# Linear attention mixer: the second value block in split form, and some low parts moved in VectorE's order

## The chip, the cores and the metric

The kernel runs on one core of one Trainium2 chip. The metric is device time in microseconds (us) of one execution, median of several; lower is better. The kernel is written by hand for the five engines: TensorE (PE), VectorE (DVE), ScalarE (ACT), GpSimd (POOL) and SyncE (SP), each with its own instruction list, ordered by semaphores. Weights come from HBM by DMAs that SP issues in a fixed order.

## What is computed

The reference is a stack of blocks on 256 tokens of width 1024 in float32: an mLSTM mixer, a mixture of experts (MoE, 16 experts), a gated linear attention mixer (GLA), a second MoE, then a pooling layer, two SwiGLU layers and an attention layer. The change is in the GLA mixer:

```
z = x @ w_in
q, k, v, r, glr = jnp.split(z, [qk, 2 * qk, 2 * qk + D_MODEL, 2 * qk + 2 * D_MODEL], axis=-1)
loga = log_sigmoid(glr @ gate_w + gate_b) / GLA_TAU
o_fwd = gla_chunked(q, k, v, loga[:, :, 0])          # A[t,s] = sum_d q k exp(b_t - b_s), then A @ v
o_bwd = flip_seq(gla_chunked(flip_seq(q), flip_seq(k), flip_seq(v), flip_seq(loga[:, :, 1])))
o = head_norm(o_fwd + o_bwd, norm_g)
return (jax.nn.silu(r) * o) @ w_out
```

## The kernel before

**Split form.** A float32 product can be made in two ways here. *Plain*: the float32 operands go to TensorE as they are; each such product of 128x512 stands as two records in the trace. *By parts*: ScalarE rounds a weight chunk (128x1024) to a high part (`hi`, line 862), VectorE subtracts to get the low part (`lo`, line 867), and TensorE adds three faster products: high by high, high by low, low by high (`PARTS`). The split activations are there from the stage's start. A chunk's parts live in one of three buffers: 0 and 1 in `w_hi`/`w_lo`, 2 in `h_hi`/`h_lo`. `hi` of a chunk waits until TensorE is done with the chunk that had its buffer (`Mixer.free`, counted by `chunk_done`), and `lo` waits for `hi`; TensorE waits for `lo` (`split_ready`).

**Value blocks.** v and r are four blocks of 512 columns, m = 0 to 3 (v, v, r, r). Each has two weight units of 1 MB (the two halves of the contraction), a unit being two chunks. `project(n)` makes half of the work of block m = n // 2. Blocks in `WHOLE_SPLIT` (0 and 3) are made by parts only, by `both_tiles`: four chunks, two for each `project`. Blocks 1 and 2 use their first unit plain (`plain_rows`, line 1847) and their second unit by parts (`split_rows`, line 1860): two chunks for the whole block. The mixer has 28 chunks: 0 to 7 for q and k, 8 to 11 block 0, 12 and 13 the second half of block 1, 14 and 15 of block 2, 16 to 19 block 3, and 20 to 27 the output product.

**Levels.** The attention matrix is built in eight levels, for distances 1, 2, 4, ... 128. For each level n, VectorE computes arguments (`args(n)`, lines 2108 and 2110), ScalarE takes their exponents (line 2032, two instructions), VectorE multiplies them with keys and queries (`key_query(n)`, line 2121), TensorE makes the small products (`level(n)`, line 1904, the last one line 1924), and VectorE copies the wanted entries (`merge(n)`, line 2129, for n < 5; later levels are merged by ScalarE). The two factors of a level lie in one of two buffers, so `args(n + 2)` waits until TensorE has made level n. VectorE's order was, for each n: `key_query(n + 1)`, `merge(n)`, `args(n + 2)`, then one or two low parts. TensorE's order is `project(n)`, `level(n)`.

**SP.** `mixer_sync` loads the mixer's 16 units, then `moe_sync(sp, 1)` follows in the same queue: it loads the next MoE's weights, 1 or 2 MB at a time, each into slots that something has to leave first. Slots of the mixer's units are left by `unit_done`; others by the end of the levels (`lv_psum`), by the head norm (`hcenter_done`), by the last chunks (`chunk_done`). From then on MoE weights stream through the same slots as its matmuls (line 1513, 1557) leave them. The queue is in order: a load that waits holds back all behind it.

Of the kernel before, what the change touches and what calls it, by code (L numbers as in the profile page):

```python
# [31 lines left out]
P = 128  # L32
SEQ, D = 256, 1024
NT = SEQ // P
KD = D // P
# [20 lines left out]
NF = D_FF // P  # L56
# [179 lines left out]
def program(nc, a, out):  # L236

    ctx = ExitStack()
    with ctx:
# [3 lines left out]
        def sem(name):  # L243
            return ctx.enter_context(nc.semaphore(name))
# [92 lines left out]
        gla_u = [st.unit((GLA_ORDER[n % 10],)) for n in range(16)]  # L337
# [16 lines left out]
        hi_ready, split_ready, chunk_done = sem("hi_ready"), sem("split_ready"), sem("chunk_done")  # L354
# [480 lines left out]
                nc.vector.tensor_tensor(xT_lo3[:, c, t], zT[:, c, t], xT_hi3[:, c, t].bitcast(F32),  # L835
                                        ALU.subtract).then_inc(xlo_ready, 1)

        MIX_CHUNKS, GLA_CHUNKS, FFN_CHUNKS = 32, 28, 3 * NF
        chunk0, chunks = {}, 0
        for name, count in (("ml", MIX_CHUNKS), ("gla", GLA_CHUNKS), ("ffn0", FFN_CHUNKS), ("att", MIX_CHUNKS),  # L840
                            ("ffn1", FFN_CHUNKS)):
# [14 lines left out]
        def split_hi(act, u, g, raw, buf, at, first=False, free=None):  # L856

            act.wait_ge(slot_landed[u.slot], u.landed_at(g))
            if not first:
                act.wait_ge(chunk_done, at - 1 if free is None else free)  # L860
            dst = split_buffer(0, buf).rearrange("p (k n) -> p k n", k=raw.shape[1])
            nc.scalar.activation(dst, raw, ACT.Copy).then_inc(hi_ready, 1)  # L862
# [6 lines left out]
        class Mixer:  # L869
# [25 lines left out]
            def hi(self, act, *chunks):  # L895
                for c in chunks:
                    split_hi(act, self.units[c // 2], 0, self.raw(c), self.buffer(c), self.at + c, first=self.at + c < 3,
                             free=self.free(c))

            def lo(self, dve, *chunks):  # L900
                for c in chunks:
                    split_lo(dve, self.raw(c), self.buffer(c), self.at + c)
# [63 lines left out]
            def token_chunk(self, pe, c, banks, operand=None, onto=False, tiles=range(NT)):  # L966

                self.products(pe, c, [(ps[banks[i]][:, :], slice(k2 * HALF, (k2 + 1) * HALF),
                                       (slice(None), c % 4 * 2 + k2, slice(i * P, (i + 1) * P)),
                                       not onto and c % 4 * 2 + k2 == 0, c % 4 * 2 + k2 == KD - 1, False)  # L970
                                      for i in tiles for k2 in range(2)], operand, more=tiles == (0,))

            def token_first(self, pe, banks, operand):
# [70 lines left out]
        ml_mix = Mixer(ml_u, 2, chunk0["ml"])  # L1044
# [642 lines left out]
        def moe_sync(sp, m):  # L1687
            def wait_slot(u):
                if u.lag is not None:
                    sp.wait_ge(unit_done, u.free_at())  # L1690
                elif u.slot == CONST_SLOT and m == 0:
                    sp.wait_ge(const_ready, 3)
                    sp.wait_ge(chunk_done, ml_mix.done(15))
                elif u.slot == CONST_SLOT:
                    sp.wait_ge(ga_psum, 1)
                elif u.slot in (SPARE_SLOT, 11):
                    sp.wait_ge(hcenter_done, HEADS * NT * (m + 1))
                    sp.wait_ge(*((num_psum, HEADS * NT), (go_psum, NT))[m])
                elif u.slot == 12:
                    sp.wait_ge(*((num_psum, HEADS * NT), (go_psum, NT))[m])  # L1700
                elif u.slot in ARENA_SLOTS and m:
                    sp.wait_ge(lv_psum, len(LEVELS))
                elif u.slot == 13:
                    sp.wait_ge(bc_psum, HEADS)
                elif u.slot == 14:
                    sp.wait_ge(gate_rows, 2)
                elif u.slot == LATE_SLOT and m == 0:
                    sp.wait_ge(cols_ready, 1)
                    sp.wait_ge(lam_ready, 1)
                    sp.wait_ge(sc_psum, HEADS)  # L1710
                elif u.slot == LATE_SLOT:
                    sp.wait_ge(lv_psum, len(LEVELS))
                elif u.slot == 10:
                    sp.wait_ge(chunk_done, (ml_mix.done(29), gla_mix.done(25))[m])
                elif u.slot in SPLIT_SLOTS:
                    sp.wait_ge(chunk_done, chunk0[("ml", "gla")[m]] + (MIX_CHUNKS, GLA_CHUNKS)[m])
                elif u.slot == XT_SLOT:
                    sp.wait_ge(xT_taken, m + 1)
# [13 lines left out]
            def load_half(u, src, h):  # L1732
                wait_slot(u)
                load(u, src[:, h * SLOT:(h + 1) * SLOT])
# [17 lines left out]
            for g in range(NGROUP):  # L1752
# [3 lines left out]
                for q in range(2):  # L1756
# [16 lines left out]
                    for c in range(2):  # L1773
# [32 lines left out]
        lv_psum, lv_done, go_psum = sem("lv_psum"), sem("lv_done"), sem("go_psum")  # L1806


        gla_mix = Mixer(gla_u[0:6] + gla_u[7:10:2] + gla_u[10:16], 2, chunk0["gla"],
                        {c: -c % 3 for c in range(10, GLA_CHUNKS)})  # L1810
        HALF_FIRST = (8, 12, 14, 16)
        WHOLE_SPLIT = (0, 3)

        def gla_tensor(pe, gen):

# [36 lines left out]
            def split_rows(n, start):  # L1852

                m, i = n // 2, n % 2
                for c in (HALF_FIRST[m], HALF_FIRST[m] + 1):
                    pe.wait_ge(split_ready, gla_mix.at + c + 1)
# [10 lines left out]
            def both_tiles(m, n):  # L1867

                c = HALF_FIRST[m] + n
                pe.wait_ge(split_ready, gla_mix.at + c + 1)  # L1870
# [10 lines left out]
            def project(n, parts=range(2)):  # L1881
                m, i = n // 2, n % 2
                if n == 6:
                    pe.wait_ge(gv_ready, 2)
                if m in WHOLE_SPLIT:
                    for part in parts:
# [67 lines left out]
        def gla_scalar(act):  # L1954
            hi = gla_mix.hi
# [58 lines left out]
            def value_rows(m):  # L2014

                if m in WHOLE_SPLIT:
                    act.wait_ge(chunk_done, gla_mix.done(HALF_FIRST[m] + 3))
                else:
                    act.wait_ge(unit_done, gla_u[5 + 2 * m].done_at())
                for i in range(NT):  # L2020
                    src = ps[V_BANKS[2 * m + i]][:, :]
                    if m < 2:
                        nc.scalar.activation(gl_v[:, i, m * HALF:(m + 1) * HALF], src, ACT.Copy).then_inc(gv_ready, 1)
                    else:
                        nc.scalar.activation(gl_r[:, i, (m - 2) * HALF:(m - 1) * HALF], src, ACT.Silu).then_inc(gr_ready, 1)
# [3 lines left out]
            for n in range(len(LEVELS)):  # L2029
                for w in range(2) if n else (1,):  # L2030
                    act.wait_ge(e_arg, n + 1)
                    nc.scalar.activation(gl_E[:, n % 2, w, :], gl_E[:, n % 2, w, :], ACT.Exp,
                                         scale=(2 * w - 1) / TAU).then_inc(e_exp, 1)
                if n == 0:
                    key_rows(1)
                    hi(act, 9, 10)
                elif n == 1:
                    hi(act, 11, 12, 13)
                elif n in (2, 4):
                    value_rows(n // 2 - 1)  # L2040
                    hi(act, 12 + n)
                elif n == 3:
                    hi(act, 15)
                elif n == 5:
                    hi(act, 17, 18)
                elif n == 6:
                    near_blocks()
                    block_merge(5)
                    hi(act, 19)
                else:  # L2050
                    block_merge(6)
                    value_rows(2)
                    block_merge(7)
                    value_rows(3)
                    hi(act, 20, 21)
            head_std(act, 1, 0)
            head_scale(act, 1, 0)
            head_std(act, 1, 1)
            zT_scalar(act, 1, 0, xT3, lambda k: mix_cols[:, 8 + k:9 + k])
            head_scale(act, 1, 1)  # L2060
            hi(act, 22)
            zT_scalar(act, 1, 1, xT3, lambda k: mix_cols[:, 8 + k:9 + k])
            hi(act, *range(23, 28))

        def gla_vector(dve, link):
            lo = gla_mix.lo
# [46 lines left out]
            def key_query(n):  # L2113
                dve.wait_ge(e_exp, 2 * n + 1)
                dve.wait_ge(gq_ready, 2)
                if n == 0:
                    factor, rows = gl_E[:, 0, 1, :], gl_q
                else:
                    dve.wait_ge(gk_ready, 2)
                    factor, rows = gl_E[:, n % 2].rearrange("p w c -> p (w c)"), gl_kq  # L2120
                nc.vector.tensor_tensor(factor, factor, rows, ALU.mult).then_inc(qd_ready, 1)
# [19 lines left out]
            for n in range(len(LEVELS)):  # L2141
                if n + 1 < len(LEVELS):
                    key_query(n + 1)
                if n < BLOCK_LEVEL:
                    merge(n)
                if n + 2 < len(LEVELS):
                    args(n + 2)
                if n < 6:
                    lo(dve, *((12, 13), (14,), (15,), (16,), (17, 18), (19,))[n])
            lo(dve, 20, 21)  # L2150
            for i in range(NT):
                dve.wait_ge(go_psum, i + 1)
                for h in range(HEADS):
# [7 lines left out]
                for h in range(1, HEADS):  # L2161
                    head_center(i, h, go_bank(i, h), gl_r)
            zT_vector(dve, 1, 0, xT3)
            lo(dve, 22)
            zT_vector(dve, 1, 1, xT3)
            lo(dve, *range(23, 28))

        def gla_sync(sp):
            mixer_sync(sp, gla_u, a["gla_w_in"][0], a["gla_w_out"][0], 2)
# [1012 lines left out]
```

## Time and profile before

| | |
|---|---|
| median of 3 runs | 1666.49 us (1665.84 to 1667.23) |
| the profiled execution | 1665.51 us, its span 1663.7 us |
| mean granted TensorE clock | 0.906 |
| busy share of the span | PE 79%, DVE 40%, ACT 27%, POOL 1% |
| HBM read | 534.17 MB, 323 GB/s over the span |
| GLA mixer | about 582 to 701 us of the span; its levels 605 to 663 us |
| second MoE | its matmuls from 718 us on |

The page gives busy time by engine and the chain of work that ended last, and the trace gives start and duration of every instruction. Start times are us from the span's start. Matmul durations are modelled and overlap, so the pace of TensorE is read from start to start; VectorE's and ScalarE's instructions overlap by about 0.1 us in the same way.

### The profile page before, as it was taken

Reading aid. Unit: us, or ns where it says so; the run is one execution under the profiler, and the core shown is the slowest. Engines: PE = TensorE matmul, PEld = TensorE weight load, DVE = VectorE, ACT = ScalarE, POOL = GpSimd, SP = SyncE. Lnnn points to the kernel's source line nnn. Section 1 sums busy time; section 2 is a strip of 40 time slices with the busy share of each in tenths; the row PEclk is TensorE's granted clock in tenths of the full one; section 3 lists DMA queues with packets and bytes.
Section 4 is the critical chain, followed back from the end, with each engine's and each line's share of the span. In section 5 each row is a group of like instructions: output and inputs, shape, how many; then the busy total and the mean of one; then the engine's idle time right before and its main releaser. Section 6 shows DMA issues by size and latency. Waiting matters only on the chain.

```text
span 1663.7 us, 20954 instructions
## 1 busy us (share of the span) xinstructions
PE 1321.7 (79%) x8638; PEld 850.4 (51%) x8638; DVE 661.7 (40%) x1083; ACT 449.0 (27%) x728; POOL 23.4 (1%) x47
## 2 busy tenths in 40 slices
PE   9999665376465899993754646669999999999997
PEld 8786121121121486841211212117888889888886
DVE  5664000000010288620100000005877678887767
ACT  4452000000000266510000000003444455654443
POOL 2000000000000100000000000000000000000000
PEclk9999887787797999997977977879999999999999
DMA  9778999999999974899999999999655763075550
GB/s 364 216 295 330 432 430 429 431 430 428 431 431 428 399 283 159 326 369 430 430 430 430 430 430 431 429 428 393 241 176 202 251 203 127 1 254 176 202 202 25
DMA packets 130856, 537.91 MB, mean 323 GB/s; under 512 B 8180, under 2 KB 71924, under 8 KB 103004
## 3 DMA queue, kind: packets, MB, share of 16 engines
q1 hardware_dynamic: 126480, 530.08, 79.7%
q10 hardware_dynamic: 2380, 2.31, 0.9%
q0 software_dynamic: 1920, 4.43, 0.8%
q8 instruction: 57, 0.93, 0.2%
q14 instruction: 19, 0.16, 0.0%
HBM read 534.17 MB, written 2.62 MB: 323 GB/s over the span
## 4 chain that ended last, share of the span: by engine, by line
PE 52%; DMA 38%; DVE 5%; ACT 2%; issue 1%; SPq 1%; DVEq 0%; ACTq 0%
PE bank L951 12%; PE bank L2355 9%; DMA ring<-in_moe_w_down 8%; DMA arena<-in_moe_w_down 7%; DMA xT_pair<-in_moe_w_up 7%; PE bank L2393 7%; DMA moe_slots<-in_moe_w_down 5%; PE bank L2359 5%; PE bank L1513 5%; PE bank L1557 5%; DMA ring<-in_moe_w_up 5%; DMA moe_slots<-in_moe_w_up 5%; DMA arena<-in_moe_w_up 2%; PE bank L589 1%; PE bank L2322 1%
## 5 line engine op out<-in xcount | busy, mean ns | idle before, releaser
L1513 PE MATMUL bank<-ring,arena 128*32 128x512 f32 x960 | 214.6, 713 | 72.5 <-DMA arena<-in_moe_w_up 36.1
L867 DVE TENSOR_TENSOR w_lo<-ring,w_hi 128x1024 fp32r<-128x1024 f32 x151 | 183.0, 1221 | 87.2 <-ACT w_hi L862 86.5
L1557 PE MATMUL bank<-ring,arena 128*32 128x512 f32 x496 | 145.3, 711 | 55.5 <-DMA moe_slots<-in_moe_w_down 22.9
L862 ACT ACTIVATE w_hi<-ring 128x1024 fp32r<-128x1024 f32 x151 | 158.6, 1057 | 82.7 <-PE bank L951 37.8
L2355 PE MATMUL bank<-xT_parts,w_hi 128*128 128x512 f32 x496 | 177.1, 399 | 0.0
L1676 DVE TENSOR_TENSOR arena<-arena,bank 64x512 f32<-64x512 f32 x32 | 22.1, 691 | 384.5 <-ACT arena L1616 384.5
L1513 PE MATMUL bank<-moe_slots,arena 128*32 128x512 f32 x352 | 104.9, 749 | 59.5 <-DMA ring<-in_moe_w_up 33.3
L2359 PE MATMUL bank<-xT_parts,w_lo 128*128 128x256 f32 x496 | 139.1, 280 | 0.0
L1513 PE MATMUL bank<-arena 128*32 128x512 f32 x488 | 106.6, 713 | 24.7 <-DMA ring<-in_moe_w_up 14.8
L1616 ACT ACTIVATE arena<-bank 64x512 f32<-64x512 f32 x32 | 18.8, 588 | 394.6 <-PE bank L1513 394.6
L1513 PEld LDWEIGHTS bank<-ring,arena 128*32 128x32 f32 x960 | 48.9, 127 | 148.4 <-issue 134.4
L1557 PE MATMUL bank<-arena 128*32 128x512 f32 x208 | 74.9, 785 | 49.5 <-DMA moe_slots<-in_moe_w_down 25.0
L2355 PEld LDWEIGHTS bank<-xT_parts,w_hi 128*128 128x128 f32 x496 | 93.2, 188 | 23.4 <-DVE w_lo L867 0.7
L1685 DVE COPY arena<-bank 128x512 f32<-128x512 f32 x8 | 5.5, 692 | 243.3 <-PE bank L1557 243.3
L1557 PE MATMUL bank<-xT_pair,arena 128*32 128x512 f32 x128 | 63.4, 708 | 45.2 <-DMA ring<-in_moe_w_down 45.2
L2359 PEld LDWEIGHTS bank<-xT_parts,w_lo 128*128 128x128 f32 x496 | 93.6, 189 | 0.7
L1624 ACT ACTIVATE arena<-bank 128x512 f32<-128x512 f32 x8 | 4.8, 597 | 317.4 <-PE bank L1557 317.4
L951 PE MATMUL bank<-w_hi,xT_parts 128*128 128x512 f32 x264 | 84.8, 395 | 1.3 <-DVE xT_parts L833 1.2
L1513 PEld LDWEIGHTS bank<-moe_slots,arena 128*32 128x32 f32 x352 | 25.5, 133 | 114.4 <-issue 112.9
L1557 PEld LDWEIGHTS bank<-ring,arena 128*32 128x32 f32 x496 | 33.2, 128 | 92.0 <-issue 89.4
L1557 PE MATMUL bank<-moe_slots,arena 128*32 128x512 f32 x160 | 73.4, 737 | 0.0
L2355 PE MATMUL bank<-xT_parts,f_hi 128*128 128x512 f32 x176 | 63.1, 398 | 0.0
(381 smaller groups left out, 2480.2 us busy)
## 6 DMA issues: line engine op xcount, KB each, us to landing
ring<-in_moe_w_up SPq DMA_DIRECT2D x24, 2048.0 KB, 38.7
ring<-in_moe_w_down SPq DMA_DIRECT2D x22, 2048.0 KB, 40.0
ring<-in_moe_w_gate SPq DMA_DIRECT2D x20, 2048.0 KB, 40.0
moe_slots<-in_moe_w_gate SPq DMA_DIRECT2D x18, 2048.0 KB, 36.9
arena<-in_moe_w_up SPq DMA_DIRECT2D x14, 2048.0 KB, 37.9
arena<-in_moe_w_gate SPq DMA_DIRECT2D x12, 2048.0 KB, 38.7
ring<-in_w_gate SPq DMA_DIRECT2D x22, 1024.0 KB, 5.1
ring<-in_w_up SPq DMA_DIRECT2D x22, 1024.0 KB, 5.2
```

The lines of the kernel that those rows point to most:

```text
L589: nc.tensor.matmul(ps[bank][:, at:at + P], ident, ident, start=True, stop=True)
L862: nc.scalar.activation(dst, raw, ACT.Copy).then_inc(hi_ready, 1)
L867: nc.vector.tensor_tensor(lo, raw, hi.bitcast(F32), ALU.subtract).then_inc(split_ready, 1)
L951: last = nc.tensor.matmul(dst, *(ops if weights_first else ops[::-1]), start=(start and p == 0), stop=(stop and p == 2))
L1513: last = nc.tensor.matmul(ps[B_GU[j % 2]][32 * c:32 * c + 32, :], xin[:, j, k, :], w, start=(k == 0), stop=(k == KD - 1), tile_position=(0 ...
L1557: last = nc.tensor.matmul(ps[B_DN[c]][32 * j:32 * j + 32, :], hT[:, j // 2, at:at + CAP], slot_row(ud[j], f % 2)[:, c * HALF:(c + 1) * HAL ...
L1616: nc.scalar.activation(hmid[64:128, j // 2, :].rearrange("p (r m) -> p r m", r=4), by_row(ps[B_GU[j % 2]][0:64, :]), ACT.Silu).then_inc(si ...
L1676: nc.vector.tensor_tensor(hmid[64 * (j % 2):64 * (j % 2) + 64, j // 2, :].rearrange("p (r m) -> p r m", r=4), hmid[64:128, j // 2, :].rear ...
L2322: return nc.tensor.matmul(FIRST_HALF[n], w[:, k * P:(k + 1) * P], x[:, k, :], start=start, stop=stop)
L2355: both = nc.tensor.matmul(gate_up_bank(f, n)[:, :], w[0][:, k * P:(k + 1) * P], xT_both[:, :, k, :], start=(k == 0), stop=False)
L2359: last = nc.tensor.matmul(gate_up_half(f, n, 1), w[1][:, k * P:(k + 1) * P], xT_hi3[:, k, :], start=False, stop=(k == KD - 1))
L2393: last = nc.tensor.matmul(acc(i, c), h_parts[hp][:, 2 * s + f, i * P:(i + 1) * P], w[wp][:, c * HALF:(c + 1) * HALF], start=False, stop=False)
```

## The change

Block 1 is made by parts as a whole, like blocks 0 and 3: its first unit is now two chunks too, 30 in all (12 to 15 are block 1, 16 and 17 the second half of block 2, 18 to 21 block 3, 22 to 29 the output). The buffers of chunks are counted from the new end, from chunk 11 on. ScalarE's list has two more high parts, and `value_rows(1)` stands after the high part of chunk 17. VectorE's list has two more low parts; those of chunks 15, 17, 19 and 21 stand right after `key_query(n + 1)`, before `merge` and `args`, for n = 2, 3, 5 and 6. The others stand after `args`.

```diff
-        MIX_CHUNKS, GLA_CHUNKS, FFN_CHUNKS = 32, 28, 3 * NF
+        MIX_CHUNKS, GLA_CHUNKS, FFN_CHUNKS = 32, 30, 3 * NF
...
             def token_chunk(self, pe, c, banks, operand=None, onto=False, tiles=range(NT)):
-                                       (slice(None), c % 4 * 2 + k2, slice(i * P, (i + 1) * P)),
-                                       not onto and c % 4 * 2 + k2 == 0, c % 4 * 2 + k2 == KD - 1, False)
+                                       (slice(None), (c - self.count) % 4 * 2 + k2, slice(i * P, (i + 1) * P)),
+                                       not onto and (c - self.count) % 4 * 2 + k2 == 0, (c - self.count) % 4 * 2 + k2 == KD - 1,
+                                       False)
...
-                    sp.wait_ge(chunk_done, (ml_mix.done(29), gla_mix.done(25))[m])
+                    sp.wait_ge(chunk_done, (ml_mix.done(29), gla_mix.done(27))[m])
...
-        gla_mix = Mixer(gla_u[0:6] + gla_u[7:10:2] + gla_u[10:16], 2, chunk0["gla"],
-                        {c: -c % 3 for c in range(10, GLA_CHUNKS)})
-        HALF_FIRST = (8, 12, 14, 16)
-        WHOLE_SPLIT = (0, 3)
+        gla_mix = Mixer(gla_u[0:8] + gla_u[9:16], 2, chunk0["gla"],
+                        {c: (GLA_CHUNKS - 1 - c) % 3 for c in range(11, GLA_CHUNKS)})
+        HALF_FIRST = (8, 12, 16, 18)
+        WHOLE_SPLIT = (0, 1, 3)
...
-                elif n in (2, 4):
-                    value_rows(n // 2 - 1)
-                    hi(act, 12 + n)
+                elif n == 2:
+                    value_rows(0)
+                    hi(act, 14)
                 elif n == 3:
-                    hi(act, 15)
+                    hi(act, 15, 16)
+                elif n == 4:
+                    hi(act, 17)
+                    value_rows(1)
                 elif n == 5:
-                    hi(act, 17, 18)
+                    hi(act, 18, 19)
                 elif n == 6:
                     near_blocks()
                     block_merge(5)
-                    hi(act, 19)
+                    hi(act, 20, 21)
                 else:
                     block_merge(6)
                     value_rows(2)
                     block_merge(7)
                     value_rows(3)
-                    hi(act, 20, 21)
+                    hi(act, 22, 23)
...
             for n in range(len(LEVELS)):
                 if n + 1 < len(LEVELS):
                     key_query(n + 1)
+                lo(dve, *{2: (15,), 3: (17,), 5: (19,), 6: (21,)}.get(n, ()))
                 if n < BLOCK_LEVEL:
                     merge(n)
                 if n + 2 < len(LEVELS):
                     args(n + 2)
-                if n < 6:
-                    lo(dve, *((12, 13), (14,), (15,), (16,), (17, 18), (19,))[n])
-            lo(dve, 20, 21)
+                lo(dve, *{0: (12, 13), 1: (14,), 2: (16,), 4: (18,), 5: (20,)}.get(n, ()))
+            lo(dve, 22, 23)
```

The remaining chunks of the output product are renumbered by two in both lists.

## Rows read from the trace of the kernel before

**Rows 1.** The page: the chain that ended last, by engine.
```profile
PE 52%; DMA 38%; DVE 5%; ACT 2%; issue 1%; SPq 1%; DVEq 0%; ACTq 0%
```

**Rows 2.** The chain that ended last, in order of time: start, length, what.
```profile
748.03 38.04 DMA ring<-in_moe_w_down
```

**Rows 3.** Timeline of VectorE: start, length, engine, line, operation, tiles, idle before.
```profile
615.48 1.23 DVE L867 TENSOR_TENSOR w_lo<-ring,w_hi 128x1024 fp32r<-128x1024 f32 x1 [1.62 <-ACT w_hi L862]
...
617.08 2.29 DVE L2121 TENSOR_TENSOR arena<-arena 128x2048 f32<-128x2048 f32 x1
...
624.16 2.28 DVE L2121 TENSOR_TENSOR arena<-arena 128x2048 f32<-128x2048 f32 x1
626.36 0.44 DVE L2129 COPY_PREDICATED glr_w<-lvl_mask,bank 128x256 f32<-128x256 uint8 x1
626.69 1.22 DVE L2108 TENSOR_TENSOR arena<-y 128x1024 f32<-128x1024 f32 x1
627.83 1.22 DVE L2110 TENSOR_TENSOR arena<-y 128x1024 f32<-128x1024 f32 x1
628.96 1.22 DVE L867 TENSOR_TENSOR w_lo<-ring,w_hi 128x1024 fp32r<-128x1024 f32 x1
631.12 2.29 DVE L2121 TENSOR_TENSOR arena<-arena 128x2048 f32<-128x2048 f32 x1 [0.94 <-ACT arena L2032]
...
649.86 2.35 DVE L867 TENSOR_TENSOR w_lo<-ring,w_hi 128x1024 fp32r<-128x1024 f32 x2
652.13 2.28 DVE L2121 TENSOR_TENSOR arena<-arena 128x2048 f32<-128x2048 f32 x1
...
658.76 2.29 DVE L2121 TENSOR_TENSOR arena<-arena 128x2048 f32<-128x2048 f32 x1 [0.94 <-ACT arena L2032]
```

**Rows 4.** Timeline of ScalarE, the same columns.
```profile
611.55 1.06 ACT L862 ACTIVATE h_hi<-ring 128x1024 fp32r<-128x1024 f32 x1 [1.26 <-PE bank L1874]
...
614.41 1.99 ACT L862 ACTIVATE w_hi<-ring 128x1024 fp32r<-128x1024 f32 x2
...
629.08 2.01 ACT L2032 ACTIVATE arena<-arena 128x1024 f32<-128x1024 f32 x2 [3.15 <-DVE arena L2110]
```

**Rows 5.** Timeline of TensorE, the same columns.
```profile
614.22 0.39 PE L1874 MATMUL bank<-w_lo,xT_parts 128*128 128x512 f32 x1
...
622.17 3.70 PE L1847 MATMUL bank<-ring,xT_pair 128*128 128x512 f32 x8
...
628.57 0.76 PE L1904 MATMUL bank<-arena 128*32 128x32 f32 x64
629.26 0.73 PE L1860 MATMUL bank<-w_hi,xT_parts 128*128 128x512 f32 x2
...
653.43 0.61 PE L1874 MATMUL bank<-w_hi,xT_parts 128*128 128x512 f32 x2
...
656.24 1.10 PE L1904 MATMUL bank<-arena 128*32 128x64 f32 x64
657.27 0.73 PE L1874 MATMUL bank<-w_hi,xT_parts 128*128 128x512 f32 x2
...
661.10 2.05 PE L1924 MATMUL bank<-arena 128*128 128x128 f32 x16 [0.82 <-DVE arena L2121]
```

**Rows 6.** Engines in a stretch: us, busy (instructions) of each, granted clock, DMA share, GB/s.
```profile
630.00:640.00 10.00, 10.00 (x91) 5.42 (x91) 8.13 (x7) 6.00 (x8) 0.00 (x0) 1.00 0.32 111
```

**Rows 7.** SP's queue: start of issue, length, engine, line, target and source, count.
```profile
635.76 0.83 SPq L1725 DMA_DIRECT2D ring<-in_moe_w_gate  x2
...
719.82 0.33 SPq L1725 DMA_DIRECT2D ring<-in_moe_w_up  x1
```

**Rows 8.** Engines in three stretches at the second MoE's start, columns as in rows 6.
```profile
716.00:720.00 4.00, 3.61 (x29) 1.87 (x28) 1.26 (x3) 0.46 (x1) 0.00 (x0) 1.00 0.27 113
...
752.00:756.00 4.00, 0.63 (x4) 0.42 (x4) 1.38 (x2) 0.01 (x1) 0.00 (x0) 1.00 1.00 430
756.00:760.00 4.00, 0.00 (x0) 0.00 (x0) 0.00 (x0) 0.00 (x0) 0.00 (x0) 0.61 1.00 426
```

More of the change, by code:

```diff
@@ L2060, in gla_scalar @@
             head_scale(act, 1, 1)
-            hi(act, 22)
+            hi(act, 24)
             zT_scalar(act, 1, 1, xT3, lambda k: mix_cols[:, 8 + k:9 + k])
-            hi(act, *range(23, 28))
+            hi(act, *range(25, 30))
         def gla_vector(dve, link):
@@ L2163, in gla_vector @@
             zT_vector(dve, 1, 0, xT3)
-            lo(dve, 22)
+            lo(dve, 24)
             zT_vector(dve, 1, 1, xT3)
-            lo(dve, *range(23, 28))
+            lo(dve, *range(25, 30))
         def gla_sync(sp):
```

## The prediction

> **What bounds the kernel now.** I read the page's chain first: half of it is TensorE, over a third DMA [rows 1]. The DMA part is the two MoEs. The chain in order of time shows where the second one turns to DMA: at 748 us TensorE starts to wait for weights [rows 2]. So the mixer counts only through the moment at which it lets that stream start, and the next view was SP's queue: the load that begins the unbroken stream is issued at 719.82, when the first MoE matmuls leave their slot [rows 7]. Just before it the DMA engines are nearly idle, share 0.27, and once the stream runs they are full, 1.00 [rows 8]. Nothing is queued there that could absorb a delay: if the mixer ends d later, the stream starts d later.
>
> Inside the mixer I read the timelines of the three engines, from start to start. VectorE and ScalarE go round one loop per level [rows 3, 4]:
> - `key_query(2)` starts at 624.16, `merge` at 626.36: 2.20;
> - `merge` to `args`, 626.69: 0.33;
> - first to second half of `args`, 627.83: 1.14;
> - to the first exponent, 629.08: 1.25;
> - two exponents until `key_query(3)`, 631.12: 2.04.
>
> Sum 6.96. Every step waits for the one before. The low part at 628.96 is in none of them: VectorE makes it while ScalarE takes exponents, and still idles 0.94. This shadow is the only place where a low part is free; it holds 1.25 - 1.14 + 2.04 = 2.15. TensorE goes round in 7.09 (622.17 to 629.26 [rows 5]) and looks just as full. Which of the two leads is read at the end of the levels: the last level product idles 0.82 and starts at 661.10, 2.34 after `key_query(7)`, which released it [rows 3, 5]. TensorE had been ready; VectorE's loop sets the end.
>
> **The change part by part.** A low part costs VectorE 1.14 from start to start (two in 2.27, 649.86 to 652.13 [rows 3]).
>
> 1. Low parts of chunks 15, 17 and 19 stand between `key_query` and `args`, in the loop itself: 3 x 1.14 = +3.41. Behind each are queued `merge`, `args` and so both exponents. Chunk 21's stands behind `key_query(7)`, with no `args` left, where VectorE had nothing to do until the levels' end: 0. Their high parts come a whole `key_query` or more earlier in ScalarE's list and their buffers are free by then, so they are not waited for.
> 2. Low parts 14, 16, 18 and 20 stand in a shadow, one each: 0. Cover gone, each would cost 1.14. Two in one shadow cost 2.27 - 2.15 = 0.12. That happened at n = 0 (still does) and at n = 4 (now one): -0.12.
> 3. Buffers. Chunk 11 now takes the buffer of chunk 9 instead of that of chunk 7, so its high part must wait for chunk 9. Chunk 9's last matmul starts at 614.22 and runs 0.39 [rows 5]; the high part of chunk 10 followed its releaser by about 0.1, so 614.71, against 614.41 before (first of the two there [rows 4]). Its low part, at 615.48, and `key_query(1)`, at 617.08, follow without a gap: +0.30. In return chunk 10's high part, held to 611.55 by 1.26 [rows 4], no longer waits; VectorE is then held by chunk 11 anyway: 0.
> 4. ScalarE gets two more high parts, 1.06 each [rows 4]. It idles 3.15 in a round [rows 4] and they stand behind the exponents: 0 for n = 3 to 5. At n = 6 both high parts and the block merges stand before the last exponents; I find them done about 0.6 before the later arguments: 0, and up to 0.5 if I am wrong.
> 5. TensorE. Block 1's plain half (8 records, 3.70 [rows 5]) goes, twice, and four chunks by parts stand in place of two. A chunk takes 2.81 (653.43 to 656.24 [rows 5]); a round of two and a level product is 2 x 2.81 + 0.69 (628.57 to 629.26 [rows 5]) = 6.3 instead of 7.09, so 0.8 less, twice. But plain products needed no split, and these do: chunk 12 starts when its low part is ready, about 623.5 instead of 622.17. By the same reckoning TensorE waits 1.3, 0.7 and 1.6 before chunks 12, 14 and 15, then 1.1 and 1.5 before chunks 18 and 19. Its gain is spent on waits: 0 on the path so far.
>
> At the last level the two sides meet. VectorE's: 0.30 + 3.41 - 0.12 = 3.59 late, so `key_query(7)` at 662.35 and its product possible at 664.69. TensorE's: `key_query(6)` is 0.30 + 2 x 1.14 - 0.12 = 2.46 late, at 654.59; the low part of chunk 19 starts 2.20 behind it and ends 1.22 later, at 658.01; chunk 19 takes 2.9 (with the short start-up after a wait), level 6 takes 1.03 (656.24 to 657.27 [rows 5]), chunk 20 takes 2.9: 664.9. TensorE is the later by 0.2, and the last level product moves from 661.10 to 664.9, **+3.8**.
>
> 6. Behind it every list is the same, renumbered: the last two chunks, the head norm, z, the output product with its eight chunks in the same buffers counted from the end. +3.8 carries on.
> 7. SP. Both first MoE loads went out together at 635.76, when plain block 1 ended [rows 7]. Now the first slot is left at chunk 13's first matmul, about 626.4, the second at chunk 15's, about 634.9. They start earlier, into DMA engines that have a share of 0.32 there [rows 6]: 0. Behind them SP waits for block 2, then for later events that all slip with the mixer. No load or byte is added.
>
> Sum for the profiled execution: 1665.51 + 3.8 = 1669.3; it lies 1.0 under the median of the runs, 1666.49, so the forecast is 1666.49 + 3.8 = **1670.3**, 0.23% slower.
>
> What I cannot read: what a low part costs between other instructions (lower bound 1.14 - 0.94 = 0.20 each, if an idle of 0.94 took it; upper 1.22, its whole length), so term 1 lies between 0.6 and 3.7. I take 1.14, because the shadow is behind `args` and the low part now ahead of it.
>
> The Trainium skill gives VectorE's full rate as 245.76 G elements/s (Perfetto Trace Analysis, Engine Utilization). By that a low part of 128x1024 would be an estimated 0.53 us and the sum about +1.9, no measurable change; the trace does not agree, the instruction takes 1.22 [rows 3].
>
> **The rivals.**
>
> *TensorE leads, and its gain counts.* For it: TensorE is busy 10.00 of 10.00 where VectorE is busy 8.13 [rows 6], and its round, 7.09, is the longer. Then the low parts ahead of `merge` are the right cure, for they feed it sooner, and two rounds lose 0.8 each: 1666.5 - 1.6 = 1664.9, 0.1% less, not slower. It decides if the last level product had not waited; it waited 0.82 for VectorE [rows 5], so TensorE would have to be later there by more than 0.8. 5 in 100, and 4 more for a gain over 0.2%, for which I find no place. The Trainium skill calls the engine with the highest occupancy the most contended, but says that matmul busy share is no good measure and to take the weight loads' (Perfetto Trace Analysis, Identifying the Most-Contended Engine); here these are 5.42 of 10, under VectorE's 8.13, so by that rule too TensorE has room [rows 6].
>
> *The stream absorbs the delay.* The MoE is DMA-bound, and two slots are refilled earlier. If loads of the 700s already stood in a queue, the end would stay at 1666.5. Against it: share 0.27 just before the stream begins [rows 8]. Full absorption 8; a part of it, or a smaller term 1, ending at 1667.5 to 1669.8: 23.
>
> *TensorE's clock falls.* It waits some 6 us in five pieces between 622 and 661. The granted clock fell to 0.61, on the way to 1.2 GHz, only behind nearly four idle microseconds at 752 to 756 and more idle behind them [rows 8]; my pieces are under 1.7 each. If it did, one chunk by parts would take up to 2 x 2.81: 1670.3 + 2.8 = 1673. 5.
>
> **How the numbers follow.** About 0.2% (3.3 us) is what a measurement of this kernel tells from no change. Forecast (1669.8 to 1671.5) 55; clock 5; absorbed in part 23; absorbed 8; TensorE leads 5; faster otherwise 4. Slower 0.60, same 0.36, faster 0.04. The range runs from full absorption, 1666.3, to 1672.0: the forecast with the upper bounds of terms 1 and 4 (1670.3 + 0.3 + 0.5) and the 0.7 by which the runs shown lie above their median. It leaves out the clock, TensorE's lead and the gain, 14.
>
> **What would show it.** Right: `key_query(7)` of the changed kernel some 3.6 later, counted from `key_query(0)`; rounds of 8.1 where chunk 15's and 17's low parts stand, 6.96 where not; VectorE idle about 2 before the `key_query` that follows the empty shadow at n = 3; TensorE idle before chunks 12, 14, 15, 18, 19 with clock 1.00; the first MoE stream load near 723.6. Wrong: rounds still near 7 (term 1), an earlier last level product (TensorE led), or a stream that starts at 719.8 in spite of it.

## The result, and the profile after

The changed kernel takes 1670.39 us (median of 14 runs, 1669.29 to 1671.93); the kernel before, 1666.45 us in the same comparison (14 runs, of which one took 4342.93 us and stands outside the ratio). The ratio is 1.0023, 95% interval 1.0016 to 1.0030: slower by 3.9 us, where 3.8 was forecast. The profiled execution of the changed kernel took 1669.8 us, its span 1668.0 us.

Lines behind 970 have moved by one to four: `key_query` is now line 2125, the two halves of `args` 2112 and 2114, `merge` 2133, the exponents 2033, `both_tiles` 1875, a plain product 1848, the level products 1905 and 1925. In this execution `key_query(0)`, which the change doesn't touch, starts at 606.05, in that of before at 605.71; this 0.34 comes from ahead of the mixer (TensorE's lines at 578 us are as late). So stage times below are counted from `key_query(0)`.

VectorE's timeline after, which answers to [rows 3] (start, length, engine, line, tiles, idle before):

```profile
616.15 1.23 DVE L867 TENSOR_TENSOR w_lo<-ring,w_hi 128x1024 fp32r<-128x1024 f32 x1 [3.12 <-ACT w_hi L862]
...
617.74 2.29 DVE L2125 TENSOR_TENSOR arena<-arena 128x2048 f32<-128x2048 f32 x1
...
631.78 2.29 DVE L2125 TENSOR_TENSOR arena<-arena 128x2048 f32<-128x2048 f32 x1 [0.94 <-ACT arena L2033]
633.99 1.22 DVE L867 TENSOR_TENSOR h_lo<-ring,h_hi 128x1024 fp32r<-128x1024 f32 x1
635.13 0.43 DVE L2133 COPY_PREDICATED glr_w<-lvl_mask,bank 128x256 f32<-128x256 uint8 x1
...
639.88 2.29 DVE L2125 TENSOR_TENSOR arena<-arena 128x2048 f32<-128x2048 f32 x1 [0.93 <-ACT arena L2033]
...
647.99 2.29 DVE L2125 TENSOR_TENSOR arena<-arena 128x2048 f32<-128x2048 f32 x1 [2.08 <-ACT arena L2033]
...
654.96 2.29 DVE L2125 TENSOR_TENSOR arena<-arena 128x2048 f32<-128x2048 f32 x1 [0.94 <-ACT arena L2033]
...
662.73 2.29 DVE L2125 TENSOR_TENSOR arena<-arena 128x2048 f32<-128x2048 f32 x1 [0.94 <-ACT arena L2033]
```

The low part of chunk 15, at 633.99, stands between `key_query` and `merge`, and the round in which it stands takes 8.10 (631.78 to 639.88); chunk 17's takes 8.11; the round with low parts in the shadow only takes 6.97. The 2.08 idle before 647.99 is the empty shadow of n = 3.

TensorE's timeline after, which answers to [rows 5]:

```profile
623.83 0.72 PE L1875 MATMUL bank<-h_hi,xT_parts 128*128 128x512 f32 x2 [1.25 <-DVE h_lo L867]
...
630.90 0.73 PE L1875 MATMUL bank<-w_hi,xT_parts 128*128 128x512 f32 x2 [0.67 <-DVE w_lo L867]
...
635.27 0.73 PE L1875 MATMUL bank<-h_hi,xT_parts 128*128 128x512 f32 x2 [1.35 <-DVE h_lo L867]
...
654.16 0.70 PE L1875 MATMUL bank<-h_hi,xT_parts 128*128 128x512 f32 x2 [1.05 <-DVE h_lo L867]
...
658.44 0.74 PE L1875 MATMUL bank<-w_hi,xT_parts 128*128 128x512 f32 x2 [1.29 <-DVE w_lo L867]
...
665.31 1.95 PE L1925 MATMUL bank<-arena 128*128 128x128 f32 x16
```

TensorE waits five times for a low part, before chunks 12, 14, 15, 18 and 19, 5.6 us in all; before the last level product, where it used to wait, it no longer does. Its clock stays full in these stretches, one of the emptiest being the first below, and the MoE stream finds the DMA engines as idle as before (columns as in rows 6):

```profile
632.00:636.00 4.00, 2.65 (x12) 1.90 (x11) 4.00 (x4) 1.65 (x2) 0.00 (x0) 1.00 0.00 0
```

```profile
720.00:724.00 4.00, 3.61 (x29) 1.87 (x28) 1.35 (x4) 0.46 (x1) 0.00 (x0) 1.00 0.29 123
```

SP's queue after, to be held against [rows 7], and the place where the chain turns to DMA, against [rows 2]:

```profile
627.07 9.07 SPq L1726 DMA_DIRECT2D ring<-in_moe_w_gate  x2
...
723.93 0.33 SPq L1726 DMA_DIRECT2D ring<-in_moe_w_up  x1
```

```profile
752.14 38.01 DMA ring<-in_moe_w_down
```

Of the two early slots the first is refilled at 627.07 instead of 635.76; the second load of the pair is issued by 636.14, about where both were. It brings nothing: the first load of the stream comes 3.77 later, counted from `key_query(0)` (117.88 against 114.11), and so does the turn to DMA.

### The profile page after: what moved, and what is told of

Read it like the earlier page. It is cut to its first block, busy times and chain, and to the rows that moved or that the text cites. A ratio compares the mean times of both kernels' runs of the same rounds, so it can differ in the third digit from the quotient of the medians.

```text
span 1668.0 us, 20976 instructions
## 1 busy us (share of the span) xinstructions
PE 1324.8 (79%) x8646; PEld 851.3 (51%) x8646; DVE 664.5 (40%) x1085; ACT 450.8 (27%) x730; POOL 23.4 (1%) x47
## 4 chain that ended last, share of the span: by engine, by line
PE 53%; DMA 38%; DVE 4%; ACT 2%; issue 1%; SPq 1%; ACTq 0%; DVEq 0%
PE bank L951 12%; PE bank L2359 9%; DMA ring<-in_moe_w_down 8%; DMA arena<-in_moe_w_down 8%; DMA xT_pair<-in_moe_w_up 7%; PE bank L2397 7%; DMA ring<-in_moe_w_up 6%; PE bank L1514 5%; DMA moe_slots<-in_moe_w_down 5%; PE bank L2363 5%; PE bank L1558 4%; DMA moe_slots<-in_moe_w_up 4%; PE bank L589 1%; PE bank L2326 1%; PE bank L1875 1%
## 5 line engine op out<-in xcount | busy, mean ns | idle before, releaser
L1514 PE MATMUL bank<-moe_slots,arena 128*32 128x512 f32 x352 | 108.3, 770 | 55.3 <-DMA ring<-in_moe_w_up 33.0
L1558 PE MATMUL bank<-moe_slots,arena 128*32 128x512 f32 x160 | 74.3, 746 | 0.0
```

Source lines behind the costliest of these rows:

```text
L1514: last = nc.tensor.matmul(ps[B_GU[j % 2]][32 * c:32 * c + 32, :], xin[:, j, k, :], w, start=(k == 0), stop=(k == KD - 1), tile_position=(0 ...
L1558: last = nc.tensor.matmul(ps[B_DN[c]][32 * j:32 * j + 32, :], hT[:, j // 2, at:at + CAP], slot_row(ud[j], f % 2)[:, c * HALF:(c + 1) * HAL ...
```

## The experiments

The same three marks for all, in us from `key_query(0)` of one profiled execution each (where `key_query` is two instructions, the start of the first); the times are medians of 5 to 14 runs, and the ratios compare them with the kernel before, run alongside (1666.45 to 1666.50).

| kernel | `key_query(7)` | last level product | first stream load | time | ratio (95%) |
|---|---|---|---|---|---|
| before | 53.05 | 55.39 | 114.11 | 1666.5 | |
| changed | 56.68 | 59.26 | 117.88 | 1670.39 | 1.0023 (1.0016 to 1.0030) |
| e1, low parts behind `args` | 58.49 | 61.94 | 120.55 | 1671.74 | 1.0030 (1.0017 to 1.0042) |
| e7, e1 with its clock kept | 55.80 | 59.25 | 117.85 | 1669.75 | 1.0019 (1.0010 to 1.0028) |
| e2, before, order alone | 56.36 | 58.70 | 119.04 | 1670.88 | 1.0025 (1.0016 to 1.0034) |
| e3, changed, other buffer rotation | 55.13 | 57.68 | 116.32 | 1668.43 | 1.0011 (1.0002 to 1.0020) |
| e5, three low parts on GpSimd | 58.54 | 60.88 | 119.82 | 1672.75 | 1.0042 (1.0029 to 1.0056) |
| e4, changed, factors in halves | 52.63 | 55.98 | 114.61 | 1666.98 | 1.0003 (0.9994 to 1.0012) |
| e6, before, factors in halves | 50.22 | 54.42 | 113.02 | 1665.41 | 0.9990 (0.9981 to 0.9999) |
| e8, e4 and e3 together | 51.04 | 54.34 | 112.96 | 1665.47 | 0.9993 (0.9984 to 1.0002) |

**e1: all low parts back behind the arguments.** If the new order alone were at fault, this would give the time back.

```diff
                     key_query(n + 1)
-                lo(dve, *{2: (15,), 3: (17,), 5: (19,), 6: (21,)}.get(n, ()))
...
-                lo(dve, *{0: (12, 13), 1: (14,), 2: (16,), 4: (18,), 5: (20,)}.get(n, ()))
+                lo(dve, *{0: (12, 13), 1: (14,), 2: (15, 16), 3: (17,), 4: (18, 19), 5: (20,), 6: (21,)}.get(n, ()))
```

> The changed kernel with all low parts back behind the arguments, in the shadow of the exponents (15 and 16 for n = 2, 18 and 19 for n = 4). Theory A (the two sides are tied: VectorE's loop pays for low parts ahead of the arguments, TensorE pays by waiting when they come later): key_query(4) comes about 1.0 us earlier than in the changed kernel, but chunk 15 starts some 2.5 us later and TensorE then sets the last level product, within 0.3 us of the changed kernel; the kernel stays about 3.7 us slower than before, 1670.2. Rival B (the new order alone is at fault): the 3.4 us come back, 1667.0. Rival C (TensorE leads anyway and the early low parts fed it): slower than the changed kernel, by 1 to 3 us.

`key_query(4)` is 0.96 earlier than in the changed kernel and chunk 15 starts 2.65 later, as theory A had it. But the kernel is not faster than the changed one, so rival B falls: e1's median is 1.4 above, with intervals that overlap, and in its profile, of an execution 1.0 above that median, the last level product is 2.7 later. Theory A had not expected these 2.7, rival C had: so the cause had to be found. TensorE's timeline and two stretches of e1:

```profile
638.24 1.22 PE L1875 MATMUL bank<-h_hi,xT_parts 128*128 128x512 f32 x2 [3.95 <-DVE h_lo L867]
...
643.65 0.95 PE L1905 MATMUL bank<-arena 128*32 128x32 f32 x64
```

```profile
634.00:638.00 4.00, 0.28 (x2) 0.00 (x0) 4.00 (x5) 0.94 (x2) 0.00 (x0) 0.92 0.00 0
638.00:642.00 4.00, 3.77 (x9) 3.03 (x10) 3.52 (x3) 2.03 (x3) 0.00 (x0) 0.50 0.47 135
```

The wait for chunk 15's low part is 3.95, and behind it the granted clock is 0.50 (0.70 already in the last microsecond of the wait), the 1.2 GHz level: chunk 15 takes 5.41 (638.24 to 643.65) instead of 2.81. VectorE then waits for the level product (3.15 before its `merge`).

**e7: the same, with TensorE kept busy over that wait.** This tells the clock from the order of the waits.

```diff
                     for part in parts:
+                        if n == 3 and part:
+                            pe.wait_ge(gv_ready, 2)
+                            keep_clock(4, 16)
                         both_tiles(m, 2 * i + part)
```

> Run e1 (all low parts behind the arguments) with 16 small matmuls more, of no use to the result, put between chunks 14 and 15, where TensorE idled 3.95 us in e1 and its clock then stood at 0.50, so that chunk 15 took 5.4 us instead of 2.8. Theory A with the clock as what e1 added: chunk 15 takes 2.8 to 2.9 us again, the last level product comes within 0.5 us of the changed kernel's, and the time falls from 1671.7 to about 1670.4. If the excess of e1 was not the clock but the order of the waits, it stays at 1671 to 1672.

```profile
633.61 3.73 PE L589 MATMUL bank<-cst 128*128 128x128 f32 x32
637.73 0.72 PE L1875 MATMUL bank<-h_hi,xT_parts 128*128 128x512 f32 x2 [0.38 <-DVE h_lo L867]
...
640.69 0.76 PE L1908 MATMUL bank<-arena 128*32 128x32 f32 x64
```

Chunk 15 takes 2.96, the last level product comes at 59.25, against 59.26 in the changed kernel. The clock is what e1 added, so rival C has nothing to stand on, and without it both orders end the levels at the same time: with the low parts ahead VectorE's loop is late (56.68 + 2.34 = 59.02), with them behind TensorE is (VectorE's side would allow 58.14). Block 1 by parts costs this much in either order, with these buffers. (The 0.6 between the two kernels' medians lies within their intervals.)

**e2: the order alone, in the kernel before.** Block 1 stays half plain.

```diff
+                lo(dve, *{2: (15,), 3: (16,), 4: (17,)}.get(n, ()))
                 if n < BLOCK_LEVEL:
                     merge(n)
...
-                if n < 6:
-                    lo(dve, *((12, 13), (14,), (15,), (16,), (17, 18), (19,))[n])
+                lo(dve, *{0: (12, 13), 1: (14,), 4: (18,), 5: (19,)}.get(n, ()))
```

> The kernel before, block 1 half plain as it was, with only the order changed: the low parts of chunks 15, 16 and 17 stand ahead of merge and arguments for n = 2, 3 and 4. Theory A: three rounds of the loop take 8.1 us instead of 6.96, the second low part of n = 4 leaves its shadow (-0.1), so key_query(7) comes 3.3 us later, the first load of the MoE stream too, and the time is 3.3 us above before, 1669.8. Rival C (TensorE leads): its chunks get their low parts earlier, so no later than before, 1666.5 or less. Rival D (the DMA stream absorbs a delay of the mixer): the mixer ends 3.3 us later, the kernel at 1666.5 to 1667.5.

`key_query(7)` is 3.31 later, as expected to the tenth. But the stream starts 4.93 later and the time is 1.1 above what was expected. TensorE's timeline of e2:

```profile
658.56 1.10 PE L1904 MATMUL bank<-arena 128*32 128x64 f32 x64 [1.45 <-DVE arena L2121]
...
665.19 3.68 PE L1924 MATMUL bank<-arena 128*128 128x128 f32 x16 [2.59 <-DVE arena L2121]
668.53 0.80 PE L1874 MATMUL bank<-h_hi,xT_parts 128*128 128x512 f32 x2
```

```profile
664.00:668.00 4.00, 2.81 (x13) 2.81 (x14) 1.14 (x1) 2.41 (x4) 0.00 (x0) 0.67 0.00 0
```

The last product takes 3.34 from its start to that of the next instruction; before, the stream load followed its start by 58.72, here by 60.34. TensorE had waited 1.45 and then 2.59, and the granted clock in the stretch is 0.67. It is 0.50 from 666 to 668. So 1.5 of the 4.93 is the clock again, by these rows; no run of this order with TensorE kept busy tells it from another cause. Rival C, that low parts ahead feed TensorE, falls: `level(1)` to `level(5)` are where they were, since half-plain blocks wait for nothing. Rival D falls too: the stream passes the delay on.

**e3: another rotation of the buffers.** Chunk 11 gets the buffer that chunk 8 left (and chunk 12 that of chunk 9).

```diff
-                        {c: (GLA_CHUNKS - 1 - c) % 3 for c in range(11, GLA_CHUNKS)})
+                        {c: (GLA_CHUNKS - 1 - c) % 3 for c in range(14, GLA_CHUNKS)})
```

> The changed kernel, but the buffers are counted from the end only from chunk 14 on, so chunk 11 takes the buffer of chunk 8 and its high part waits for nothing but the exponents. Theory A: key_query(1) comes 1.0 us earlier than in the changed kernel, and nothing later gives it back, so the last level product and the time are 1.0 us less, 1669.4 against 1670.4. If the buffer wait is not on the path, as the rival has it, no change.

VectorE's timeline of e3:

```profile
614.35 1.22 DVE L867 TENSOR_TENSOR h_lo<-ring,h_hi 128x1024 fp32r<-128x1024 f32 x1 [1.42 <-ACT h_hi L862]
615.63 0.42 DVE L2143 TENSOR_SCALAR glr_w<-bank 128x256 f32<-128x256 f32 x1
616.09 2.29 DVE L2125 TENSOR_TENSOR arena<-arena 128x2048 f32<-128x2048 f32 x1
```

The wait is on the path, and larger than expected: `key_query(1)` is 10.15 behind `key_query(0)`, against 11.69 in the changed kernel, 1.54 less, and that difference is still 1.58 at the last level product and 1.56 at the stream. I had held the diagonal copy (line 2143) to wait for the whole row of 128 small products; it waits for their first half only. This line alone gives back 1.6 of the 3.8 by the marks, 2.0 of the 3.9 by the times, whose intervals overlap.

**e5: low parts of chunks 15, 17 and 19 on GpSimd**, which is idle in the mixer.

```diff
+        POOL_LO = (15, 17, 19)
...
+        def gla_gpsimd(pool):
+            for c in POOL_LO:
+                at = gla_mix.at + c
...
+                pool.wait_ge(hi_ready, at + 1)
+                pool.wait_ge(split_ready, at)
...
+                nc.gpsimd.tensor_tensor(lo, raw, hi.bitcast(F32), ALU.subtract).then_inc(split_ready, 1)
```

VectorE's later low parts wait for `split_ready` as well, which keeps the count in the chunks' order.

> The changed kernel with the low parts of chunks 15, 17 and 19 made by GpSimd, so none but chunk 21's stands ahead of the arguments. Theory A: VectorE's rounds are 6.96 us again, and if GpSimd needs less than 3 us for a low part, TensorE gets it no later than now; key_query(7) comes about 3.4 us earlier than in the changed kernel, and the time is 1667.0, give or take 0.7. If GpSimd needs much longer (5 us or more), TensorE waits for it and the gain is lost. If GpSimd slows VectorE by their common access to memory, the rounds are above 6.96 while it runs.

The timelines of GpSimd and of VectorE in e5:

```profile
632.59 3.49 POOL L2186 TENSOR_TENSOR h_lo<-ring,h_hi 128x1024 fp32r<-128x1024 f32 x1 [57.61 <-ACT h_hi L862]
...
655.33 2.40 POOL L2186 TENSOR_TENSOR w_lo<-ring,w_hi 128x1024 fp32r<-128x1024 f32 x1 [10.46 <-DVE h_lo L867]
```

```profile
631.59 2.29 DVE L2125 TENSOR_TENSOR arena<-arena 128x2048 f32<-128x2048 f32 x1 [0.94 <-ACT arena L2033]
633.80 0.44 DVE L2138 COPY_PREDICATED glr_w<-lvl_mask,bank 128x256 f32<-128x256 uint8 x1
634.13 3.03 DVE L2112 TENSOR_TENSOR arena<-y 128x1024 f32<-128x1024 f32 x1
...
656.12 3.76 DVE L2125 TENSOR_TENSOR arena<-arena 128x2048 f32<-128x2048 f32 x1 [0.94 <-ACT arena L2033]
```

GpSimd's first low part takes 3.49, and the instruction of VectorE that meets it, the first half of `args`, takes 3.03 instead of 1.22: it ends 1.1 after GpSimd's does, as if begun only there. It goes both ways: GpSimd's had itself begun under `key_query`, which ran its usual 2.29 to 633.88, and ended 2.20 behind that. The low part at 655.33, which began while VectorE had nothing to do, takes 2.40, and there `key_query` takes 3.76 and ends 2.15 behind it. The Trainium skill has this as an exclusive lock on the port pair that GpSimd shares with VectorE's instructions of two inputs from SBUF (SBUF — State Buffer, SBUF: two separate sides); the trace agrees. So of the 3.49 about 1.2 looks like GpSimd's own standing still, and 2.4 is nearer to what a low part costs it. `merge`, which reads a bank, ran at its usual 0.44 at the same time. The round with this meeting is 1.8 longer (8.78 against 6.96), more than the 1.14 that was to be saved, and TensorE waits 2.43 for chunk 15's low part.

**e4, e6, e8: shortening the loop.** `key_query` in two instructions, so that the keys' half follows the first exponent.

```diff
+                if n:
+                    dve.wait_ge(e_exp, 2 * n)
+                    dve.wait_ge(gk_ready, 2)
+                    nc.vector.tensor_tensor(gl_E[:, n % 2, 0, :], gl_E[:, n % 2, 0, :], gl_k, ALU.mult)
                 dve.wait_ge(e_exp, 2 * n + 1)
+                dve.wait_ge(gq_ready, 2)
+                factor, rows = gl_E[:, n % 2, 1, :], gl_q
```

> The changed kernel with key_query in two instructions, keys and queries: the first starts after the first of the two exponents. Theory A: each level's round is shorter by the second exponent less one instruction's start, 0.9 us, except where low parts fill the shadow; key_query(7) comes about 4 us earlier than in the changed kernel, and TensorE then sets the end of the levels, at about +0.3 against the kernel before: 1666.8. If the clock falls at one of TensorE's waits, up to 2.5 more. Rival C (TensorE leads in the changed kernel too): the time stays at 1670.4.

> The kernel before with key_query in halves, block 1 half plain. Theory A: VectorE's loop loses 0.9 us where it idled, so TensorE, at 7.09 per round and never waiting, sets the end; only its 0.82 wait before the last product goes: 1665.6. Rival (VectorE's loop is the only bound): 3 us less, 1663.5.

> The changed kernel with key_query in halves and with the buffers counted from the end from chunk 14 on (runs e4 and e3 together). Theory A: the 1.6 us of e3 come on top of e4, less what TensorE's waits keep: 1665.3 to 1666. If it is under 1663.2 it is a version better than both by more than can be mistaken; I expect it within 0.1% of the kernel before.

All three times came out as expected, within 0.2. In the changed kernel (e4) it gives back 3.4 of the 3.9: VectorE's loop was its bound. Its last level product is then 0.59 behind that of before, where about 0.3 was expected. In the kernel before (e6) `key_query(7)` starts 2.83 earlier (50.22 against 53.05), and its second half, which releases the product, ends 2.8 earlier; but the last level product comes only 0.97 earlier, which is its old wait of 0.82 and little more. The second half of `key_query(7)` and TensorE's timeline of e6, which has no wait left there:

```profile
658.23 1.22 DVE L2121 TENSOR_TENSOR arena<-arena 128x1024 f32<-128x1024 f32 x1
```

```profile
657.41 1.10 PE L1904 MATMUL bank<-arena 128*32 128x64 f32 x64
...
661.29 1.95 PE L1924 MATMUL bank<-arena 128*128 128x128 f32 x16
```

e6 and e8 are 1.1 and 1.0 under the kernel before (0.1%), the lowest times of the study. e6's interval ends just under 1, e8's includes it, and both lie under what this measurement tells from no change. With the loop shortened and the rotation mended, block 1 by parts costs nothing, and gains nothing either.

## Why the prediction was right

Its forecast came true in size and in mechanism, and in one point, the clock, with some luck (below). The steps, in its own numbering:

1. Low parts ahead of `args`, +3.41 in the sum. The two rounds with chunks 15's and 17's are 8.10 and 8.11 against 6.96 [rows 3], the one with chunk 19's 7.77 against 6.63 (652.13 to 658.76 [rows 3]): 1.14, 1.15 and 1.14. e2 shows the same without the rest of the change.
2. The second low part leaving n = 4's shadow, -0.12: that round took 6.97.
3. The buffer, +0.30: chunk 11's low part and `key_query(1)` are 0.33 and 0.32 later, 617.74 - 617.08 - 0.34. Against the kernel before it was right; as something that can be undone it is worth 1.5 (e3), since the chunk then starts ahead of where it used to as well.
4. ScalarE, 0. Its last exponents had an idle of 0.51 before them, against the 0.6 that I reckoned: nearly used up, and not on the path.
5. TensorE's waits: 1.3, 0.7, 1.6, 1.1 and 1.5 were named, 1.25, 0.67, 1.35, 1.05 and 1.29 measured. The last level product is 3.87 later, where 3.8 stands in the sum (its terms give 664.84, written as 664.9), and it follows TensorE's side by 0.24, as reckoned: VectorE's would have allowed 59.02.
6. and 7. What is behind the levels passes it on: 3.77 at the first stream load. The early refill brings nothing, as reckoned.

Sum for the profiled execution: 1669.3 forecast, 1669.8 measured, of which 0.34 came in ahead of the mixer. Two slips in the working change nothing: the range's upper end adds up to 1671.8, not 1672.0, and at 748 us it is the chain that turns to DMA, while TensorE works on until 751.4 and idles for the weights from 753.5.

The rivals. That TensorE leads is refuted from both sides: e2 gives it its low parts early and it comes out slower; e6 shortens VectorE's loop and gains what TensorE had waited, though no more: behind VectorE's loop TensorE is the next bound (e4, e6). That the stream absorbs the delay is refuted by the marks of all ten kernels: the first stream load follows the last level product by 58.6 to 58.7 in eight of them, by 58.9 in e5 and by 60.3 in e2. The clock was the rival that I held too small. In the changed kernel it did not fall, with waits up to 1.35. But it fell in e1, behind a wait of 3.95, and in e2, behind 1.45 and 2.59 with 4.0 of work between them, and cost 2.6 and 1.5. The prediction took nearly four idle microseconds as what it needs, from the one place that [rows 8] show; that was one row and no bound, and in e2 less was enough. The prediction did not know how much room it had, so that the clock stayed up is in part luck.

What stays open: how near to such a fall the changed kernel is, and how much of the difference between marks and times is more than the spread of the runs: against the kernel before it is up to 0.2 in four kernels, 0.3 in e3, about 0.5 in e7, e2 and e5, and 1.2 in e1.

## What to carry to other kernels

Before a piece of work is moved ahead "because it is needed next", find which loop closes through the instructions that it is moved past. Here it was put into VectorE's and ScalarE's loop to relieve TensorE's, which had 0.8 to spare, and a shadow of 2.15 stood half empty behind it. Filling the shadow instead was no cure: TensorE then waited for the late low part, and the levels ended at the same time (e7). What helped was a shorter loop (e4) and another buffer (e3). Two loops of 6.96 and 7.09 are both bounds: speeding TensorE up by 0.8 a round was worth nothing while its new operands came through the other loop. And a wait of TensorE costs more than its length once its clock falls, so a plan that leaves TensorE with waits of 1.5 to 4 us has a second price to look up in the granted clock.

## What the hardware showed

- GpSimd's 128x1024 float32 subtraction took 2.40 us where it began with VectorE idle, and 3.49 and 3.51 where it began while VectorE's `key_query` ran; VectorE's own takes 1.22. VectorE's instruction with two SBUF inputs stood still while GpSimd's ran (3.03 and 3.04 instead of 1.22, 3.76 instead of 2.29), one that reads a bank did not (0.44).
- The granted clock stood at the 1.2 GHz level, 0.50, behind one idle of 3.95 us (e1), and fell to it (0.67 in the mean of four microseconds, 0.50 in two of them) behind 2.59 us that followed 1.45 us (e2); it stayed at 1.00 over five idles of 0.67 to 1.35 us in 36 us (changed kernel).
- A chunk of twelve 128x512 products took 5.41 us at the lower clock, 2.81 at the full one.
